# A two-block transformer kernel on one core: the first modulation vectors in four column quarters instead of two halves

## What is computed

```python
mod = (jax.nn.silu(c) @ w_ada[l] + b_ada[l])              # c: 2048, w_ada: 2048 x 12288
shift1, scale1, gate1, shift2, scale2, gate2 = split(mod, 6)
h = rms_norm(x, norm1_w[l]) * (1.0 + scale1) + shift1
proj = h @ w_in[l]                                        # 2048 x 7168
aq, ak, av, gq, gf, gi, gg = split(proj, ...)             # 3 x 1024 attention, 4 x 1024 HGRN2
attn = dilated_attention(rope(rms_norm(aq)), rope(rms_norm(ak)), av)
ho = hgrn2(gq, gf, gi, lb)
x = x + gate1 * (concat(rms_norm(attn), rms_norm(ho) * silu(gg)) @ w_out[l])
x = x + gate2 * (square(relu((rms_norm(x) * (1 + scale2) + shift2) @ w_ff1)) @ w_ff2)
...                                                       # second block: stick-breaking attention, MLP
```

## Time and profile before

| | |
|---|---|
| median of 3 runs | 2432.97 us (2432.86 to 2433.14) |
| the profiled execution, its own time | 2433.19 us |
| its span, first to last instruction | 2431.4 us |
| PE busy in the span | 97% |
| DVE, ACT, POOL busy | 66%, 43%, 2% |
| mean granted TensorE clock | 0.988 |

### The profile page before, as it was taken

How to read it: one execution, slowest core, us unless ns; L and a number is a source line. 1 busy time by engine, 2 the same in 40 slices (tenths; PEclk the granted TensorE clock), 3 DMA queues, 4 the chain that set the end, 5 groups by cost and what they waited for, 6 DMA issues and landing times.

```text
span 2431.4 us, 27934 instructions
## 1 busy us (share of the span) xinstructions
PE 2359.0 (97%) x10954; PEld 1968.0 (81%) x10954; DVE 1594.6 (66%) x1284; ACT 1039.6 (43%) x890; POOL 51.4 (2%) x56
## 2 busy tenths in 40 slices
PE   4899999999999999999999999999999999999999
PEld 3777888887888888888887888878888888888887
DVE  7868989987666666655568456556555565565554
ACT  2245553435333333333334556664443433433432
POOL 1011000001000000000000000000000000000000
PEclk9789999999999999999999999999999999999999
DMA  9988987755676776655554545444555655555552
GB/s 355 362 300 311 361 311 268 252 199 169 231 241 231 234 242 224 224 190 181 183 190 171 177 160 168 156 138 158 183 191 183 191 184 192 189 188 190 190 189 104
DMA packets 235129, 520.30 MB, mean 214 GB/s; under 512 B 9705, under 2 KB 10162, under 8 KB 232370
## 3 DMA queue, kind: packets, MB, share of 16 engines
q1 hardware_dynamic: 234352, 519.15, 63.2%
q10 hardware_dynamic: 706, 0.17, 0.0%
HBM read 517.19 MB, written 2.10 MB: 214 GB/s over the span
## 4 chain that ended last, share of the span: by engine, by line
PE 90%; DVE 4%; DMA 2%; ACT 2%; issue 1%; DVEq 1%; POOL 1%; ACTq 0%; SPq 0%
PE PS L257 28%; PE PS L259 28%; PE PS L258 28%; DMA ada_raw<-in_w_ada_dram 2%; PE PS L1695 2%; PE PS L1734 1%; PE PS L1669 1%; DVE w_lo L247 1%; PE PS L306 1%; ACT w_hi L243 1%; POOL rstd L609 1%; PE PS L1679 1%; DVE ada_acc L1144 0%; DVEq L1511 0%; PE PS L1799 0%
## 5 line engine op out<-in xcount | busy, mean ns | idle before, releaser
L247 DVE TENSOR_TENSOR w_lo<-raw,w_hi 128x2048 fp32r<-128x2048 f32 x392 | 897.6, 2291 | 688.4 <-ACT w_hi L243 683.4
L243 ACT ACTIVATE w_hi<-raw 128x2048 fp32r<-128x2048 f32 x392 | 750.9, 1916 | 1149.1 <-PE PS L259 1137.7
L257 PE MATMUL PS<-w_hi,A_hi 128*128 128x512 f32 x2112 | 839.7, 398 | 10.0 <-DVE A_lo L361 3.5
L259 PE MATMUL PS<-w_hi,A_lo 128*128 128x512 f32 x2112 | 827.5, 392 | 0.0
L258 PE MATMUL PS<-w_lo,A_hi 128*128 128x512 f32 x2112 | 827.2, 392 | 0.0
L257 PEld LDWEIGHTS PS<-w_hi,A_hi 128*128 128x128 f32 x2112 | 400.6, 190 | 92.2 <-ACT qT L738 2.8
L259 PEld LDWEIGHTS PS<-w_hi,A_lo 128*128 128x128 f32 x2112 | 399.5, 189 | 84.9
L258 PEld LDWEIGHTS PS<-w_lo,A_hi 128*128 128x128 f32 x2112 | 400.4, 190 | 81.2 <-issue 1.0
L257 PE MATMUL PS<-w_hi,H_hi 128*128 128x512 f32 x1024 | 401.6, 392 | 2.0 <-issue 1.3
L259 PE MATMUL PS<-w_hi,H_lo 128*128 128x512 f32 x1024 | 398.9, 390 | 0.0
L258 PE MATMUL PS<-w_lo,H_hi 128*128 128x512 f32 x1024 | 398.5, 389 | 0.0
(11 more groups left out here) (267 smaller groups left out, 1108.0 us busy)
## 6 DMA issues: line engine op xcount, KB each, us to landing
raw<-in_w_ff_dram SPq DMA_DIRECT2D x128, 1024.0 KB, 5.3
raw<-in_mlp_w_in_dram SPq DMA_DIRECT2D x64, 1024.0 KB, 5.4
raw<-in_mlp_w_out_dram SPq DMA_DIRECT2D x64, 1024.0 KB, 5.0
raw<-in_w_in_dram SPq DMA_DIRECT2D x56, 1024.0 KB, 8.1
X<-in_w_ada_dram SPq DMA_DIRECT2D x96, 512.0 KB, 5.7
raw<-in_sb_w_qkv_dram SPq DMA_DIRECT2D x48, 1024.0 KB, 5.1
ada_raw<-in_w_ada_dram SPq DMA_DIRECT2D x32, 1024.0 KB, 9.8
raw<-in_w_out_dram SPq DMA_DIRECT2D x16, 1024.0 KB, 6.6
```

The costliest lines, as they stand in the source:

```text
L243: act.activation(w_hi[:, j, :, :], raw[:, j, :, :], ACT.Copy).then_inc(hi_rdy, 1)
L247: dve.tensor_tensor(w_lo[:, j, :, :], raw[:, j, :, :], w_hi[:, j, :, :].bitcast(F32), ALU.subtract).then_inc(lo_rdy, 1)
L257: pe.matmul(bank(pair + t), h, w_hi[:, j, k, :], start=first, stop=False)
L259: mm = pe.matmul(bank(pair + t), l, w_hi[:, j, k, :], start=False, stop=last)
```

## The change

**Quarters.** The pieces become 128 rows by 512 columns of shift1 and scale1 (512 KB), 16 for each of four column quarters (q), in eight slots of the same memory (`RING`). `quarter_sums` and `quarter_modulation` take the place of `step_sums`, `direct_sums` and `step_modulation`; PE takes pieces 3, 7, 11 in quarter 0 and 11, 13, 15 in quarters 1 to 3. Slots 0 to 11 now go by quarter: chunks 3q, 3q+1, 3q+2 are the Q, K and V columns of channel blocks 4q to 4q+3. Ten `w_in` chunks are loaded and split between the pieces, before it was eight.

**Third chunk.** In quarters 1 and 2 PE runs the third chunk of the quarter before between `quarter_sums` and the second transposing step. A first chunk of a quarter (b = 0) waits for `A_lo` step by step.

**Masks and root.** ACT squares X with a running sum (L827 of the changed kernel); POOL draws the level masks; the attention masks move to DVE's slots 10 and 11 (`counts`, `masks`).

**After the opening.** The first group's Q is ready for its square sum with chunk 9, K with chunk 10 (it was 7 and 9), so squares, norm, transposes and copies of that group move to slots 10 to 13, its transposes go to banks 6 and 7, and its attention stages run one slot later (`STAGE_LAG`). Slot 12 waits for the multiplied Q instead of its copy. The ring pieces start at slot 10, two a slot, with three in slots 13, 21, 36, 37, 49, 50.

```diff
-ADA_BY_PE = (3, 7, 11), (7, 11)
-LOADS_AFTER = {(0, 9): 0, (0, 11): 1, (0, 13): 2, (1, 0): 3, (1, 2): 4, (1, 4): 5, (1, 6): 6, (1, 9): 7}
+QUARTERS = D // NC_
+RING = 2 * CH
+AT0_ORDER = [(b, k) for k in range(QUARTERS) for b in range(3)]
+HEAD = 3 * (QUARTERS - 1)
+ADA_BY_PE = (3, 7, 11), (11, 13, 15), (11, 13, 15), (11, 13, 15)
+STAGE_LAG = 1
+LOADS_AFTER = {(0, 9): 0, (1, 0): 1, (1, 6): 2, (1, 10): 3, (2, 0): 4, (2, 5): 5, (2, 10): 6, (3, 0): 7, (3, 5): 8, (3, 10): 9}
+LOW_AFTER = {(0, 12): 0, (1, 4): 1, (1, 9): 2, (1, 14): 3, (2, 4): 4, (2, 9): 5, (2, 14): 6, (3, 4): 7, (3, 9): 8, (3, 14): 9}
+ADA_FROM = HEAD + 1
+ADA_THREE = 13, 21, 36, 37, 49, 50
...
 @@ scalar
+            act.wait_ge(x_in, 16)
+            for t in range(T):
+                act.activation(Y0[:, t, :], X[:, t, :], ACT.Square, accum_out=ssq[:, t:t + 1]).then_inc(row_sq, 1)
             act.wait_ge(rstd_rdy, POWER_OF[0])
             for c in range(4):
                 normalise(act, X, X, c)
...
+            split_hi(act, 0, 0)
+            for q in range(QUARTERS):
+                turn_act(act, 0, g1, mod[:, SHIFT1, :], turned, steps=(2 * q, 2 * q + 1), first=2 * q, banks=QUARTER_BANKS)
+                for n in range(3 * q + 1, 3 * q + 4):
+                    split_hi(act, n // CH, n % CH)
...
 @@ vector
+            for q in range(QUARTERS):
                 for k in range(KT):
+                    if k in ADA_BY_PE[q]:
                         continue
...
+                        ins = dve.scalar_tensor_tensor(out=acc, in0=sl, scalar=sc[:, k:k + 1], in1=acc, op0=ALU.mult, op1=ALU.add)
                     ins.then_inc(ada_used, 1)
...
+                    if (q, k) == (0, 8):
                         first_root()
+                    if q and k == 0:
+                        quarter_modulation(q - 1)
+                    if q and k in (1, 2):
+                        turn_first(2 * (q - 1) + k - 1)
...
+                    if i == 0 and s == HEAD + 1:
+                        counts()
+                    if i == 0 and s == HEAD + 2:
+                        masks()
+                    if i == 1:
+                        at_own(0, PROJ0, CH * 3 + s, True)
...
 @@ tensor
+            for q in range(QUARTERS):
+                for k in ADA_BY_PE[q]:
+                    piece_sums(q, k)
+                pe.wait_ge(y_rdy, q + 1)
+                turn(0, X, steps=(2 * q,), first=2 * q, banks=QUARTER_BANKS[:1])
+                quarter_sums(q)
+                if q in (1, 2):
+                    at0_chunk(pe, 3 * q - 1)
+                pe.wait_ge(mod_rdy, q + 1)
+                turn(0, X, steps=(2 * q + 1,), first=2 * q + 1, banks=QUARTER_BANKS[1:])
+                for n in ((0, 1), (3, 4), (6, 7, 8), ())[q]:
+                    at0_chunk(pe, n)
...
-        return {"square": (8, 10), "norm": (9, 11), "turn": (10, 12), "copy": (11, 12)}
+        return {"square": (10, 11), "norm": (11, 12), "turn": (12, 13), "copy": (13, 13)}
```

More of the change, by code:

```diff
@@ L120 @@
 PIECES_BEFORE = {0: 0, 1: 4, 2: 6}
+QUARTER_BANKS = 6, 7
 MIX_JOBS = 2 + HG_GROUPS + 2 * AT_GROUPS
@@ L193, in build @@
         small = turned[:, :, :].rearrange("p a n -> p (a n)")
+        ada_slots = ada_raw[:, :, :].rearrange("p j (h n) -> p (j h) n", n=2 * NC_)
+        ada_sum_of = [setup[:, D + 2 * NC_ * i:D + 2 * NC_ * (i + 1)] for i in range(2)]
         PS = ctx.enter_context(nc.psum_tensor("PS", [P, 8, NC_], F32))
@@ L281, in at0_chunk @@
             b, k = AT0_ORDER[n]
[L282 to L285, removed]
+            if b:
+                chunk(pe, n // CH, n % CH, pairs[b], lambda i, t: A_hi[:, CH * k + i, P * t:P * t + P],
+                      lambda i, t: A_lo[:, CH * k + i, P * t:P * t + P], k == 0, k == CH - 1)
+                return
+            j = n % CH
+            pe.wait_ge(lo_rdy, n + 1)
+            for i in range(CH):
+                if i % 2 == 0:
+                    pe.wait_ge(a_lo, 2 * k + i // 2 + 1)
+                for t in range(T):
+                    h, l = (x[:, CH * k + i, P * t:P * t + P] for x in (A_hi, A_lo))
+                    first, last = k == 0 and i == 0, k == CH - 1 and i == CH - 1
+                    pe.matmul(bank(pairs[b] + t), h, w_hi[:, j, i, :], start=first, stop=False)
+                    pe.matmul(bank(pairs[b] + t), h, w_lo[:, j, i, :], start=False, stop=False)
+                    mm = pe.matmul(bank(pairs[b] + t), l, w_hi[:, j, i, :], start=False, stop=last)
+            mm.then_inc(chunk_done, 1)
         def a_chunk(pe, B, j, pair, turned=None, tokens=range(T)):
@@ L458, in _ @@
             ada = a["w_ada"].rearrange("a (k p) (s n) -> p (a k) s n", p=P, n=D)
[L459 to L471, removed]
+            for piece in range(QUARTERS * KT):
+                q, k = divmod(piece, KT)
+                if piece >= RING:
+                    q0, k0 = divmod(piece - RING, KT)
+                    if k0 in ADA_BY_PE[q0]:
+                        sp.wait_ge(ada_pe, ada_share(q0, k0, True))
+                    else:
+                        sp.wait_ge(ada_used, ada_share(q0, k0, False))
+                sp.dma_start(ada_slots[:, piece % RING, :].rearrange("p (s n) -> p s n", s=2),
+                             ada[:, k, 0:2, NC_ * q:NC_ * (q + 1)]).then_inc(ada_in[piece % RING], 16)
+                if (q, k) == (0, CH - 1):
+                    sp.dma_start(X[:, :, :], a["x"].rearrange("a (t p) d -> p (a t) d", p=P)).then_inc(x_in, 16)
+                if (q, k) in LOADS_AFTER:
+                    load_at0(LOADS_AFTER[q, k])
             for n in range(len(LOADS_AFTER), CH * 3):
@@ L1075, in step_modulation, with turn_first @@
                                          op0=ALU.add, op1=ALU.mult).then_inc(g_rdy, 1)
-            def turn_first(steps, first, **more):
-                turn_dve(dve, 0, g1, mod[:, SHIFT1, :], turned, steps=steps, first=first, **more)
-            for h in range(2):
+            def turn_first(step):
+                turn_dve(dve, 0, g1, mod[:, SHIFT1, :], turned, steps=(step,), first=step,
+                         banks=QUARTER_BANKS[step % 2:step % 2 + 1], tmp_at=step % 2)
+            for q in range(QUARTERS):
@@ L1332, in at_stage @@
                     dve.tensor_tensor(AMf[:, 0:384], AMf[:, 384:768], bank(7, 0, 384), ALU.subtract).then_inc(arg_rdy, 1)
-            split_lo(dve, 2, 0)
-            turn_first(ALL[6:], 6)
+            for step in (KT // 2 - 2, KT // 2 - 1):
+                turn_first(step)
+            for n in range(len(LOW_AFTER), CH * 3):
+                split_lo(dve, n // CH, n % CH)
             dve.memset(V1_heads[:, :, :, HD:HD + 1], 1.0).then_inc(v_ones, 1)
```

259 lines of the change are left out of this document (110 added, 149 removed).

## The result

| | before | after | ratio, 95% interval |
|---|---|---|---|
| time, median of 6 runs | 2432.69 us | 2443.64 us | 1.0046, 1.0033 to 1.0059 |
| span of the profiled execution | 2431.4 us | 2441.7 us | |

The changed kernel is 11 us slower, against a forecast of 2430.0 us, and outside the range up to 2437.5. It does start its large work 27 us earlier, as meant; what it lost lies between that start and slot 9, and in slots 10 to 26. The difference is small, 0.46%, but the interval is clear of 1.

The account below looks back on a forecast made before the run. PE is 97% busy but DVE walks right beside it, so an earlier PE gains only what DVE can follow. From 2432.97, less 3.8 us gained by slot 26, plus a 1 us stall: 2430.0 us, range 2418 to 2437.5.

Parts of the forecast that it names:

- Durations: Prices used throughout the walk: 8 one-column matmuls 1.75 us on an idled PE, 24 right behind chunks 3.1 us.
- Quarter 0: First column quarter: DMA sets the pace up to piece 12, DVE's part ends at 43.9, slot 0 starts at 49.1 us.
- T1: Moment when quarter 0's gain is ready, after sums of 1.85 and modulation of 0.7 us: 46.5 us.
- the new wait for ScalarE: Quarter 0: DVE, done with piece 12 at 34, waits 3.5 us for ACT to split chunk 0.
- The second new wait: Quarters 2 and 3: DVE waits 3.7 us each because the second step's transposes stand behind the third chunk on PE.
- T3: End of quarter 2 in the walk, with the second new wait and 2.2 us for bounds and angles: 105.0 us.
- Quarter 3: Last quarter: DVE's last piece at 131.1, DVE waits 5 us for PE, modulation done at 140, slot 9 starts at 142.7.
- Slots 9 to 26: DVE gives back 8.3 us of its 11.5 us lead to masks, Q's square sum and rotation; PE gains 3.8 us.
- After slot 26: PE stays 3.8 us ahead, then DVE's third pieces in slots 36 and 37 make a slot 41 stall of some 1 us.
- Rival B: Lead eaten: gain zero if chunk 12's `w_lo` ends at 155.0, each later us lost; 2433 to 2437 us, chance 0.18.
- Rival C: Smaller transfers are slower, so DMA bounds the opening below some 375 GB/s; 2438 us at 350 GB/s, chance 0.06.
- Rival A: DVE keeps up, opening at DMA pace, slot 9 at 127: 2415 to 2420 us, 0.10; partial form 2423 to 2428, 0.24.

Follow-up runs that it names:

- the run without them: Changed kernel with pair counts and masks moved from DVE's slots 10 and 11 to behind piece 2 of quarter 0; 2440.00 us.
- the run with the second step first: Changed kernel with the third chunk of quarters 1 and 2 put behind the second step's transposes on PE; 2433.75 us.
- the run with one piece: Changed kernel, masks behind quarter 0's piece 2, third chunk behind second step's transposes, PE summing only piece 3 of quarter 3, between chunks 6 and 7; 2425.27 us.
- the run with the early sums: Changed kernel with PE summing pieces 3, 6 and 8 of quarter 3, between chunks 6, 7 and 8, instead of 11, 13 and 15; 2435.06 us.

## Why the prediction was wrong

**The step that failed is the price of the one-column matmuls**, given under "Durations": "32 one-column matmuls take 6.99 us on a PE that has idled, so 8 take 1.75; right behind chunks 4.18, so 24 take 3.1". The x32 in the earlier trace rows counts records, and a float32 one-column matmul leaves two of them. The program of before has 16 in each of those places (`for c in range(KT)` in `piece_sums`); that of after has `for c in range(8)`, so 8 for a quarter's sum and 24 for three pieces, where the profile shows x16 and x48. So eight cost 3.5 us and not 1.75, and 24 cost 7.05 and not 3.1. Both durations were read rightly; the count beside them was not compared with the loop in the code. The trace of before had the right price as well: in half 1 `step_sums` takes eight columns at a time, and these are its rows, at the upper and at the lower clock:

```profile
127.05 1.84 PE L1679 MATMUL PS<-ones,MS 128*128 128x1 f32 x16
...
131.66 3.57 PE L1679 MATMUL PS<-ones,MS 128*128 128x1 f32 x16 [1.41 <-ACT A_hi L347]
```

Point by point:

- **Quarter 0**, forecast T1 46.5, measured 48.8. VectorE's part ended at 44.4 (43.9): X landing, the root, ScalarE's normalising and the new wait for ScalarE (1.96 us instead of 3.5) came within 2 us. The sums took 3.57 instead of 1.85.
- **Quarters 1 and 2.** The second new wait was foreseen, 3.7 us each; it was 5.37 and 5.04, since the sums in front of it ended later and the chunk took 7.9 and 7.6 us, not 7.2. T3 110.4 against 105.0. Chunk 8 starts at 133.81 against 127.1, so 6.7 of the 13 us had gathered by then.
- **Quarter 3**, the rest: behind chunk 8 I had 3.1 + 0.5 + 1.3 us, measured 7.05 + 0.9 + 3.4. That is 6.4 us more. VectorE's wait there was 12.53 us, forecast 5. Slot 9: 155.70 against 142.7, **13.0 us late**.
- **Slots 9 to 26.** Forecast: 8.3 us given back. Measured: 7.1 (114.3 against 107.2). That these are near each other is in part luck. The terms that the forecast names come to 9.5 (6.7 + 2.7, and twice 3.1 - 1.14 - 1.9), not to 8.3, and with 9.5 it would have been 1.2 us higher; and VectorE's waits from chunk 12's `w_lo` to slot 26 fell from 9.3 to 7.5 us in all, 1.3 of it a wait for ScalarE's `w_hi` that is gone. The masks count 3.3 in the run without them, not 6.7, since behind them VectorE waits for ScalarE's Q. The rotation's wait was 2.9 (forecast 3.1), and TensorE's waits before the P transposes of slots 15 and 19 are 2.61 and 2.47 (forecast 2.5 each).
- **After slot 26.** The stall in slot 41 is there and is 0.8 us (forecast 1; the earlier trace rows). The sum had nothing for the clock behind slot 26's wait. TensorE waits 2.63 us there for ScalarE's exponential and starts the P transposes at 280.83, 7.9 us later than before; then its granted clock is 0.50 from 281 to 284 us, where before it stayed at 1.00, and at the tenth matmul behind them it is 9.6 us late. So 7.9 + 1.6 + 0.8 make the 10.3 us of the span.
- **Rival B** had the mechanism: from 155.0 on, each us by which chunk 12's `w_lo` ends later is a us lost. It ended at 164.97; 2432.97 + 9.97 is 2442.9, measured 2443.6. I gave B 0.18 and ended it at 2437, by naming causes of 2 to 5 us and none of 13.
- **Rival C**, small transfers being slower, is out: the DMA moved 404 and 405 GB/s from 80 to 120 us in the run with the second step first. The Trainium skill (DMA: Bandwidth & Descriptors, section Bandwidth) says to batch transfers to 1 MiB or more for 75% of the peak or more; the forecast's estimate from it had the last piece 24 us late. No such lateness shows in this queue of 512 KB pieces and 1 MB chunks, and the measured rate decides.
- **Rival A** did not happen in the change. Even the run with one piece starts slot 9 at 141.51, and gains 7.3 us. A slot 9 at 127 was reached by no run, so what it would give is not shown.

What I had not asked at all is whether a predicted wait could be ordered away. The two waits "behind the third chunk" stood in my sum as facts; the run with the second step first shows that they were worth 9 us at the price of 1.2.

With the count put right and nothing else, the forecast would have been about 2440, an estimate worked out afterwards: 3.2 us more for the 24 piece sums of quarter 3 (6.3 for 3.1), 1.3 for its sum (2.6 for 1.3) and 1.75 in each of the three quarters before are 9.7 us at slot 9, on a walk that had room for 3.0. The other 3.3 of the 13.0 us are roughly these, most of it the clock: 7.05 + 3.4 + 0.9 in quarter 3, where the corrected terms have 9.4, and the two chunks in front of the second steps, 1.1 longer; 0.5 was VectorE's part in quarter 0. No run tests this division; the run with the early sums shows 2.5 us of clock in quarter 3.
